# State-space inputs gathered in pairs and used before the Toeplitz kernels, modulation columns one tile later, query spread behind the last state group

## What is computed

```python
z = x @ w_in[i]
xs, gs, cq, ckv, kr, gm = jnp.split(z, IN_SPLIT_POINTS, axis=-1)
ys = s5_branch(xs, a_re[i], a_im[i], log_dt[i], b_re[i], ...) * jax.nn.silu(gs)
ym = mla_branch(cq, ckv, kr, cos, sin, q_norm_g[i], w_uq[i], kv_norm_g[i], w_ukv[i]) * jax.nn.silu(gm)
...
# s5_branch: 32 groups of 16 channels, 64 complex states each
_, _, h_re, h_im = lax.associative_scan(combine, (a_seq_re, a_seq_im, x_re, x_im), axis=0)
y = einsum('gcp,lbgp->blgc', c_re, h_re) - einsum('gcp,lbgp->blgc', c_im, h_im)
y = y.reshape(bsz, seqlen, SSM_WIDTH) + d_skip * uf
```

## Time and profile before

| | us |
|---|---|
| median of 3 runs | 2229.31 |
| lowest and highest run | 2228.81, 2230.44 |
| the profiled execution | 2233.53 |
| its span, first to last instruction | 2231.7 |
| PE busy in the span | 2122.7 (95%) |
| DVE, POOL, ACT busy | 1226.7, 1235.6, 777.9 |

### The profile page before, as it was taken

The page is one execution under the profiler, slowest core; times in us unless marked ns, Lnnn a source line. Parts: engine busy times, 40 slices in busy tenths (PEclk is TensorE's granted clock), DMA queues, the critical chain, the costliest instruction groups (busy, mean ns, idle before and its releaser), DMA issues.

```text
span 2231.7 us, 28169 instructions
## 1 busy us (share of the span) xinstructions
PE 2122.7 (95%) x11208; PEld 1656.5 (74%) x11208; DVE 1226.7 (55%) x1476; ACT 777.9 (35%) x1188; POOL 1235.6 (55%) x826
## 2 busy tenths in 40 slices
PE   8969989999998999999999999998999999999998
PEld 3757853887885886568857788876788888888886
DVE  6994965651577214520068425766866666652424
ACT  6212142332115204630064443144554545531211
POOL 1582640318882673336647664473788888844441
PEclk9979999999998999999999999999999999999999
DMA  7462461014322321101211235223122222154112
GB/s 282 142 127 76 130 184 62 10 68 169 104 85 67 141 76 60 31 20 57 71 23 70 90 114 198 86 113 141 38 85 85 85 85 85 57 177 154 48 38 75
DMA packets 66033, 212.68 MB, mean 95 GB/s; under 512 B 15159, under 2 KB 17511, under 8 KB 64719
## 3 DMA queue, kind: packets, MB, share of 16 engines
q1 hardware_dynamic: 52624, 152.73, 20.3%
q10 hardware_dynamic: 9040, 36.45, 4.4%
q0 software_dynamic: 4240, 21.70, 3.6%
HBM read 162.73 MB, written 46.17 MB: 94 GB/s over the span
## 4 chain that ended last, share of the span: by engine, by line
PE 83%; DVE 7%; ACT 3%; POOL 2%; issue 2%; DMA 2%; SPq 0%; ACTq 0%; DVEq 0%
PE ps L3292 22%; PE ps L2903 16%; PE ps L3411 11%; PE ps L2925 6%; PE ps L3216 4%; PE ps L3325 3%; PE ps L2868 3%; PE ps L3363 2%; PE ps L355 2%; PE ps L525 1%; PE ps L513 1%; PE ps L378 1%; PE ps L1036 1%; PE ps L507 1%; PE ps L538 1%
## 5 line engine op out<-in xcount | busy, mean ns | idle before, releaser
L1579 POOL TENSOR_TENSOR w_parts<-front,sb_zero 128x1024 fp32r<-128x1024 f32 x69 | 140.4, 2034 | 282.6 <-PE ps L3411 117.7
L1654 POOL TENSOR_TENSOR up_parts<-front,up_parts 128x512 fp32r<-128x512 f32 x120 | 194.4, 1627 | 69.5 <-ACT up_parts L1956 69.4
L3411 PE MATMUL ps<-ffn_parts,w_parts 128*128 128x512 f32 x1008 | 230.3, 389 | 1.5 <-DVE front L2829 1.5
L1584 POOL TENSOR_TENSOR w_parts<-front,w_parts 128x1024 fp32r<-128x1024 f32 x75 | 208.0, 2774 | 22.8 <-ACT w_parts L2111 7.5
L3411 PEld LDWEIGHTS ps<-ffn_parts,w_parts 128*128 128x128 f32 x1008 | 189.0, 188 | 41.7 <-issue 2.6
L3292 PE MATMUL ps<-t_high,up_parts 128*128 128x512 f32 x640 | 204.9, 391 | 5.2 <-ACT back L1963 5.2
L2903 PE MATMUL ps<-h_high,w_parts 128*128 128x512 f32 x672 | 187.6, 394 | 0.6 <-PE ps L3216 0.6
L3292 PE MATMUL ps<-h_high,up_parts 128*128 128x512 f32 x480 | 154.6, 389 | 1.5 <-DVE back L2597 1.5
L3292 PEld LDWEIGHTS ps<-t_high,up_parts 128*128 128x128 f32 x640 | 120.8, 189 | 31.2 <-issue 6.0
L1472 POOL TENSOR_TENSOR front<-front,sb_csilu 128x1024 f32<-128x1024 f32 x48 | 103.5, 2156 | 72.4 <-DMA front<-w_ada 72.4
L2903 PEld LDWEIGHTS ps<-h_high,w_parts 128*128 128x128 f32 x672 | 124.0, 188 | 25.8 <-issue 1.4
(11 more groups left out here) (429 smaller groups left out, 4889.4 us busy)
## 6 DMA issues: line engine op xcount, KB each, us to landing
front<-w_ada SPq DMA_DIRECT2D x48, 512.0 KB, 3.6
front<-w_up SPq DMA_DIRECT2D x44, 512.0 KB, 4.4
front<-w_down SPq DMA_DIRECT2D x22, 512.0 KB, 3.5
front<-w_in SPq DMA_DIRECT2D x16, 512.0 KB, 3.7
front<-w_out SPq DMA_DIRECT2D x16, 512.0 KB, 4.9
residual<-back ACTq DMA_DIRECT2D x2, 4096.0 KB, 15.5
front<-w_gates SPq DMA_DIRECT2D x16, 512.0 KB, 4.0
gates<-back SPq DMA_DIRECT2D x16, 512.0 KB, 3.6
```

What stands on the lines that cost most here:

```text
L1579: pool.tensor_tensor(high, raw, zero[:, 0:1].to_broadcast((P, PAGE)), ALU.add)\
L1584: pool.tensor_tensor(low, raw, high.bitcast(F32), ALU.subtract).then_inc(S("w_split"), 1)
L1654: pool.tensor_tensor(parts[:, BANK:], src, parts[:, 0:BANK].bitcast(F32), ALU.subtract)\
L3411: mm = pe.matmul(ps[:, 2 * m + nt, :], parts[n % 2 + w_][:, at:at + P], half_of(AR[kk % 4 + x_], nt), start=k == 0 and q == 0, stop=k == N ...
```

## The change

Four things are done.
1. POOL issues the eight gathers of UU in pairs: two after `in_low(7)`, two after `ada_sum(4)`, two after `in_low(8)`, two after `ada_sum(5)`, where all eight stood after `in_low(7)`.
2. The state inputs (now x = 16 to 23, counted as the second eight) stand before tile 9, the Toeplitz kernels behind it, on PE and in ACT's copies. DVE starts its scans after the state inputs and makes the skip term between its two halves.
3. ACT rounds block 9 behind the copies of the transposes and no longer between gates 6 and 7. Pages are reassigned for that: block 9 goes to page 22 and block 11 waits for tile 9 to be done.
4. The modulation column i-3 that tile i carried is column i-4 now; tile 5 has none, tile 15 two. The spread of the query norm stands behind round 3, not behind round 2.

```diff
             elif i in (10, 11):
...
+            elif i in (9, 10):
                 act.wait_ge(S("ssm_ps"), 8)
+            elif i == 11:
+                act.wait_ge(S("z_tile"), 10)
             elif i in (12, 13):
-                act.wait_ge(S("ssm_ps"), 24)
+                act.wait_ge(S("ssm_ps"), 16)
...
+            def gather(s):
+                pool.dma_start(UU[s * GC:(s + 1) * GC, :, :],
+                               x_dram.rearrange("(g c) t -> c g t", c=GC)[:, :, s * CHUNKS:(s + 1) * CHUNKS])\
+                    .then_inc(S("u_landed"), 16)
...
             for i in range(6, N_IN):
                 ada_sum(i - 4)
+                if i in (8, 9):
+                    gather(4 * i - 30)
+                    gather(4 * i - 29)
                 if i == 9:
                     pool.wait_ge(S("z_tile"), 8)
                     pool.memset(TM, 0.0).then_inc(S("pool_step"), 1)
...
-                    for s in range(STEP):
-                        pool.dma_start(UU[s * GC:(s + 1) * GC, :, :],
...
+                if i in (7, 8):
+                    gather(4 * i - 28)
+                    gather(4 * i - 27)
...
             for tile in range(4, 8):
                 gate(tile)
-                if tile < 7:
+                if tile < 6:
                     in_high(act, tile + 3)
...
+            in_high(act, 9)
             in_high(act, 10)
             gate(8)
+            act.wait_ge(S("gate_out1"), 32)
+            for x in range(16, 24):
...
+            gate(9)
+            in_high(act, 11)
...
-                in_products(bank, (IN_HIGH[i],), XH, between={0: 0, 4: 1} if i == IN_FIRST else {0: i - 3})
+                in_products(bank, (IN_HIGH[i],), XH, between={4: {0: 0, 4: 1}, 5: {}, 15: {0: 11, 7: 12}}.get(i, {0: i - 4}))
...
-                elif r == 2:
+                elif r == 3:
                     latent_spread_pe(pe, "q_norm")
```

More of the change, by code:

```diff
@@ L1761, in _ @@
                     .then_inc(S("ssm_ps_read"), 1)
[L1762 to L1770, removed]
             in_high(act, 12)
@@ L2350, in _, with skip @@
             dve.sem_inc(S("dve_step"), 1)
-            dve.wait_ge(S("ssm_ps_read"), 16)
[L2353 to L2362, removed]
+            def skip():
+                dve.wait_ge(S("ssm_ps_read"), 24)
+                dve.wait_ge(S("consts_landed"), 64)
+                dg = cols(_bc, _bc + GROUPS * GC, GC).rearrange("p (g c) -> p g c", g=GROUPS)
+                tt(dg, ident[0:GC, 0:GC].unsqueeze(1).to_broadcast((GC, GROUPS, GC)),
+                   dsk[0:GC, :].unsqueeze(2).to_broadcast((GC, GROUPS, GC)), ALU.mult)
+                tt(GSB[:, :, 0:GC], GSB[:, :, 0:GC], dg, ALU.add)
+                dve.sem_inc(S("dve_step"), 1)
+            T1, T2 = (page(a).rearrange("p (q n) -> p q n", q=PAIRS // 2) for a in (32, 33))
+            dve.wait_ge(S("ssm_ps_read"), 16)
             S0, S1 = SS[:, 0], SS[:, 1]
@@ L2365, in _ @@
             for half in range(2):
+                if half:
+                    skip()
                 qs = slice(half * PAIRS // 2, (half + 1) * PAIRS // 2)
@@ L2973, in _ @@
             in_tile(8)
+            pe.wait_ge(S("u_landed"), 16 * STEP)
+            for x in range(16, 24):
+                pe.wait_ge(S("ssm_ps_read"), x - 9)
+                q4, i = (x - 16) // 2, x % 2
+                for j in range(4):
+                    q = 4 * q4 + j
+                    for g2 in range(2):
+                        mm = pe.matmul(ps[64 * g2:64 * g2 + 64, 5 + x % 2, j * P:(j + 1) * P],
+                                       PW[:, q, i, 64 * g2:64 * g2 + 64], UU[:, 2 * q + g2, :],
+                                       start=True, stop=True)
+                mm.then_inc(S("ssm_ps"), 1)
+            in_tile(9)
             pe.wait_ge(S("dve_step"), DVE_STEP["cp_table"])
             for x in range(8, 16):
-                pe.wait_ge(S("ssm_ps_read"), x - 1)
+                pe.wait_ge(S("ssm_ps_read"), x + 7)
                 r, odd = (x - 8) // 2, x % 2
@@ L2983, in _ @@
                                        CP[h, i, q, 0:P], start=i == 0, stop=i == 1)
-                mm.then_inc(S("ssm_ps"), 1)
-            in_tile(9)
-            pe.wait_ge(S("u_landed"), 16 * STEP)
-            for x in range(16, 24):
-                pe.wait_ge(S("ssm_ps_read"), x - 1)
-                q4, i = (x - 16) // 2, x % 2
-                for j in range(4):
-                    q = 4 * q4 + j
-                    for g2 in range(2):
-                        mm = pe.matmul(ps[64 * g2:64 * g2 + 64, 5 + x % 2, j * P:(j + 1) * P],
-                                       PW[:, q, i, 64 * g2:64 * g2 + 64], UU[:, 2 * q + g2, :],
-                                       start=True, stop=True)
                 mm.then_inc(S("ssm_ps"), 1)
```

17 lines of the change are left out of this document (9 added, 8 removed).

## The result

| | kernel before | changed kernel |
|---|---|---|
| median of the runs, us | 2229.88 (4 runs, 2228.81 to 2231.21) | 2211.85 (4 runs, 2211.12 to 2214.04) |
| ratio, 95% interval | | 0.9907 (0.9891 to 0.9922) |
| the profiled execution | 2233.53 | 2214.04 |
| its span | 2231.7 | 2211.3 |

A forecast was written before the change was run, and what follows sets the result against it. The prediction took PE to be the bound, with its idle and half-clock time as the gain to win. Its four terms, 2.8 + 10.8 + 3.2 + 2.0 = 18.8 us, took the median from 2229.3 to 2210.5, range 2204.5 to 2219.

The forecast's parts named there:

- What bounds the kernel: PE, busy 95% of the span; an edit is worth the PE idle or half-clock time it removes, longest wait 12.0 us.
- Term 1: Tiles 5 to 7: modulation columns a tile later save 2.8 us, with 5.0 us idle left ahead of tile 6 for in_low(6).
- Term 2: Transposes ahead of tile 8: rounding block 9 behind the copies saves 10.8 us.
- Term 3: Tiles 8 to 10: state inputs ahead of the Toeplitz kernels save 3.2 us, 3.9 less 0.6 to 0.7 lost.
- The sum: 2.8 + 10.8 + 3.2 + 2.0 = 18.8 us gained, taking the median from 2229.3 to 2210.5.
- UU in time: State inputs: UU needed at 165.2; fourth pair issued behind ada_sum(5) at 152, last pair landing near 160, 5 us early.
- Term 4: Key spread to values: query spread behind round 3 saves 2.0 us (0.6 + 1.4), limited by the scatter of y.
- the upper end: Spread term's upper case, 4.4 us: the full 6.1 less the longer wait for DVE in the key tiles.
- The rule that speaks against it: Tiles 11 to 14: later w_ada loads leave POOL 18.6 us; beside DVE's big table operations it could need 20.9.
- the rivals: Alternative totals: more comes through 2205.4 (0.12), UU late 2216.5 (0.15), POOL bound 2217.5 (0.07), copies still wait 2221.3 (0.03), slower 2240 (0.03).

The follow-up runs named there:

- late_round10: all_but_swap with ACT's rounding of block 10 moved from ahead of gate 8 to behind the Toeplitz kernels' copies; 2219.99 us, ratio 0.9945 to the kernel before.
- low_both: Changed kernel with in_low(6) and in_low(7) ahead of ada_sum(2) and ada_sum(3) on POOL, columns 2 and 3 later in tiles 6 and 7; 2212.96 us, ratio 0.9918.
- round9_alone: Kernel before with one edit: ACT rounds block 9 behind the copies of the transposes; 2222.11 us, ratio 0.995.
- changed_again: The changed kernel itself, unaltered, timed once more against the kernel before; 2212.85 us, ratio 0.991.
- pairs_alone: Kernel before with one edit: POOL issues the gathers in pairs; 2226.49 us, ratio 0.9977.
- spread_round2: Changed kernel with the query norm's spread put back behind round 2; 2215.92 us, ratio 0.9919 to the kernel before.
- both_and_at_once: low_both with all eight gathers behind ada_sum(3), TM zeroed behind in_low(9), blocks 9 and 10 rounded among and behind state-input copies; 2212.27 us, ratio 0.9908.
- columns_alone: Kernel before with one edit: tile i carries modulation column i-4; 2232.66 us, ratio 1.000.
- columns_back: Changed kernel with the modulation columns back where they stood, column i-3 in tile i; 2217.37 us, ratio 0.993 to the kernel before.
- low_first: Changed kernel with in_low(6) ahead of ada_sum(2) on POOL and column 2 at tile 6's eighth product; 2212.47 us, ratio 0.9911 to the kernel before.
- all_but_swap: Kernel before with pairs, columns, block 9 and spread edits, but Toeplitz kernels still ahead of tile 9 and state inputs behind it; 2220.00 us, ratio 0.9945.

## Why the prediction was right, by its own steps

- **What bounds the kernel: shown.** Taking block 9 out of ACT's way, one line, removed the 12 us wait.
- **Term 1, 2.8 us: right in mechanism, small in size.** The stop ahead of tile 6 was 5.2 us and POOL's `in_low(6)` its cause, as written. It measured 4.0 because the clock took 1.5 us behind it (5.28 us for a low part of 3.79), and I had charged 2.5. What the term did not say is its condition: over the stretch it is 0.3 alone and 3.4 in the changed kernel.
- **Term 2, 10.8 us: right in mechanism, small in size; measured 12.2.** For the edit alone the stretch shrank by 10.7: 12.0 by tile 8, less 1.3 lost again at the state inputs. Tile 8 came 5.9 us behind tile 7's end, where I had kept 7.2 from a passage at half clock; at full clock PE waits 1.30, 0.20 and 0.20 us for the copies.
- **Term 3, 3.2 us: right; measured 4.0** (3.7 by late_round10). The state inputs took 7.8 us, not 8.5. The first copy was 0.33 us late, not 0.5, and the Toeplitz kernels lost 0.6 as written. That DVE hides now (its reciprocal ends at 254.26, 6.7 us ahead of the key spread, 1.5 before) is worth another 3.3 us that would be lost without the swap. The sum counts those 3.3 us in terms 1 and 2.
- **UU in time: right.** The fourth pair was issued at 147.95, where I had 152, and the gathers' queue moved nothing after 157, so some 4.5 us were to spare. They are no fixed slack: in low_both PE came at 155.97, the last gather landed at 162.4, since the loads issued at 149 took 38.9% and 65.7% of the engines ahead of it (152 to 157, 157 to 162), and PE stood 6.4 us.
- **Term 4, 2.0 us: right size, wrong reason.** It measured 1.6, and 1.95 by the undone spread. I let it be cut by the scatter of y. The scatter's read-back was issued 4.3 us ahead of the first query rounding, since it took 16.5 us (289.95 to 306.40) and not 20 (311.82 to 331.83 before), so it did not stay on its own clock. What cut it is what I had named only for the upper end: PE waits longer for DVE's `k_low` in the key tiles, 3.98 us where it was 1.73, and its granted clock falls behind that (the first four matmuls take 3.75 us, 1.96 before). The sum had no term for that fall; the forecast of this term came near by luck:

```profile
288.00:297.00 9.00, 6.71 (x10) 0.67 1.01 231
```

- **The rule that speaks against it: did not bite.** In tiles 11 to 14 PE never waited for POOL; from tile 10 to the key spread the stretch is 0.2 us longer. POOL's slowest passage stayed beside DVE's big tables: the folds of `ada_sum(2)` took 6.50 (two) and 2.65 us (the last) there, 2.18 and 0.48 two turns later. But POOL was slower beside DVE's scans too, as POOL in order of time shows:

```profile
202.80 3.83 POOL L1478 TENSOR_TENSOR front<-front 128x512 f32<-128x512 f32 x2
206.70 1.32 POOL L1480 TENSOR_TENSOR front<-front 128x128 f32<-128x128 f32 x1
```

  An `ada_sum` and the `in_low` behind it took 10.6 us at most there (200.25 to 210.83), where they had taken 16.0 beside the tables (104.39 to 120.37) and 18.6 were allowed with the landing. The Trainium skill, in "SBUF — State Buffer", section "SBUF: two separate sides", has the shared port pair as a lock between the two engines; these rows agree with it as far as POOL is slower beside DVE's work, and don't show a lock as such.
- **The sum.** The stretch shrank by 21.6 and 20.9 us in the two traces, the medians fell by 18.0 and 18.1. So the forecast hit the median with terms that were some 2.5 us too small: the mechanisms were right, the closeness of the total is in part luck. (One slip in the rivals: 2.5 and 2.4 us off 2210.5 is 2205.6, not 2205.4.)

**What stays open** is that difference. Part of it is plain: the profiled executions differ by 19.5 us and their spans by 20.4, so 1.5 us lie in which execution was profiled. In the spans, 1.1 us were won ahead of the stretch and 2.3 lost again behind it. Nearly every kernel here shows it (round9_alone 10.7 and 10.1, late_round10 13.7 and 10.9). A part of the loss can be seen in the attention behind the stretch: PE stops for 1.85 us in the kernel before and 1.86 in changed_again at the same place, and the clock falls behind it in the one execution only. PE in order of time, before:

```profile
398.27 0.52 PE L366 MATMUL ps<-sb_ident,back 128*128 128x128 f32 x3 [1.85 <-ACT back L449]
...
399.30 0.39 PE L355 MATMUL ps<-k_low,q_high 128*128 128x512 f32 x1
```

and in changed_again:

```profile
377.12 0.56 PE L366 MATMUL ps<-sb_ident,back 128*128 128x128 f32 x3 [1.86 <-ACT back L449]
...
378.76 0.63 PE L355 MATMUL ps<-k_low,q_high 128*128 128x512 f32 x1
```

The fourteen traces say more. Ten have this stop, of 1.85 to 1.89 us; behind it the same matmul took 0.63 us in five (both of the changed kernel, pairs_alone, spread_round2, both_and_at_once) and 0.39 or 0.40 in the other five (before, columns_alone, columns_back, low_first, low_both). The other four have a stop of 0.34 to 0.37 us there and no fallen clock. Both groups of five hold kernels with and without each edit, so the fall doesn't follow from the change, as far as one trace of each tells. The rest of the difference stays open.

## What to carry to other kernels

A wait that ends with a transfer behind a backlog hardly moves on the clock: edits ahead of it are worth little until it is gone (here 1.1 of 2.4 us came through, and 0.3 were left in the end), and edits that cure the same wait don't add up (the pairs gave 6 us alone and nothing beside the later rounding). So price a set of edits by what is late next, and test it by undoing each one in the finished kernel as well as doing each one alone. When one stop is removed, count the spare time of every other engine in that stretch (here UU had some 4.5 us and DVE's reciprocal 6.7): the smallest bounds what the next improvement can bring. An in-order engine that waits for a load ahead of work which needs no load is the cheapest thing to mend: here it was 10 of 18 us for one line.

## What the runs showed of the hardware that I had not expected

- How long a load waits behind a backlog depends on when it is issued. Behind eight gathers the software queue had 103.9% of the engines for 5 us and a load issued at their end landed after 17.55 us; from 142 to 147 us the gathers still had 104.1% and the load's queue moved nothing. In both_and_at_once the backlog was the same. A w_ada load issued at 134.96, 2 us after the first gather and ahead of most of them, took 11.7 us, and the w_in load issued 0.4 us behind it 17.4; their queue had 60.0% of the engines from 142 to 147. The Trainium skill, in "DMA: Bandwidth & Descriptors", section "Queues, rings and completion order", has each engine go round between its queues packet by packet; read plainly, that would give the load of the earlier trace rows a turn from its start, and the trace has it wait.
- Half clock can hold without a further stop. After a stop of 1.62 us, 96 small matmuls (64x16) in all_but_swap took 14.65 us; from 171 to 182 us the granted clock was 0.50, the lower of the two levels, though PE was busy all that time. The same step took 11.20 us for 128 of them in late_round10, at 1.00.
- A stop of the same length, 1.85 to 1.89 us, was followed by full clock in five executions and by half clock in five others (the attention, above). So a stop of that size can't be charged with certainty.
